# The fourth rotary embedding as four separate steps among the first half heads of the attention

## What is computed

```python
def rope_1d(x, pos):
    ...
    x1, x2 = x[..., :half], x[..., half:]
    return jnp.concatenate([x1 * cos - x2 * sin, x2 * cos + x1 * sin], axis=-1)

    qh = axial_rope(split_qk(q, S), row_pos, col_pos) * (DA_QK_DIM ** -0.5)
    kh = axial_rope(split_qk(k, S), row_pos, col_pos)
    k_all = jnp.concatenate([kh, split_qk(k_ctx, n_ctx)], axis=3)
    ...
        s = jnp.einsum('bhiqd,bhikd->bhiqk', qb, k_all).astype(jnp.float32)
        p = jax.nn.softmax(s, axis=-1)
        attn = p[:, :, 0] - lam * p[:, :, 1]
        return jnp.einsum('bhqk,bhkd->bhqd', attn.astype(v_all.dtype), v_all)
```

## Time and profile before

| | |
|---|---|
| median of three runs | 1947.11 us |
| lowest and highest | 1945.34 and 1947.85 us |
| the profiled execution, its own time | 1946.39 us |
| its span in the profile | 1944.6 us |
| instructions | 27546 |
| TensorE, VectorE, ScalarE busy | 98%, 72%, 50% of the span |

### The profile page before, as it was taken

One profiled execution on the slowest core, in us unless ns is written; L12 is line 12 of the kernel. 1 busy time (PEld: TensorE's weight loads), 2 busy tenths in 40 slices (PEclk: granted clock), 3 DMA queues, 4 the chain that ended last, 5 costly groups with the idle time before them and its releaser, 6 DMA issues.

```text
span 1944.6 us, 27546 instructions
## 1 busy us (share of the span) xinstructions
PE 1904.8 (98%) x10948; PEld 1640.9 (84%) x10948; DVE 1408.1 (72%) x1940; ACT 967.7 (50%) x1437; POOL 304.3 (16%) x490
## 2 busy tenths in 40 slices
PE   9999999999999999999999999999999999999998
PEld 8989898877888898977888888888888888888886
DVE  5686777764999989889878658666465677666665
ACT  6556566563544433444444455554443355545544
POOL 1025243342122222222221100100000000011000
PEclk9999999999999999999999999999999999999999
DMA  7455353544788888777887866765656544454563
GB/s 264 130 161 168 118 167 117 163 150 145 234 284 280 284 266 273 226 244 222 280 298 246 312 217 216 229 200 193 191 176 206 160 131 134 148 166 157 165 238 130
DMA packets 209233, 393.16 MB, mean 202 GB/s; under 512 B 12488, under 2 KB 61936, under 8 KB 207696
## 3 DMA queue, kind: packets, MB, share of 16 engines
q1 hardware_dynamic: 191248, 323.17, 50.8%
q0 software_dynamic: 17712, 68.17, 11.3%
q10 hardware_dynamic: 144, 0.07, 0.0%
HBM read 387.13 MB, written 4.23 MB: 201 GB/s over the span
## 4 chain that ended last, share of the span: by engine, by line
PE 83%; DVE 8%; issue 3%; ACT 3%; POOL 2%; DMA 1%; SPq 0%; DVEq 0%; ACTq 0%; POOLq 0%
PE GB L2121 44%; PE GB L2148 17%; PE GB L2133 9%; PE GB L2136 4%; DVE WL L2045 3%; DVE macc L1385 1%; PE SB L403 1%; ACT WH L2040 1%; PE SB L1693 1%; POOL XB L1069 1%; PE SB L1794 1%; PE SB L1685 1%; PE SB L1801 1%; POOL TB L1066 1%; PE SB L805 1%
## 5 line engine op out<-in xcount | busy, mean ns | idle before, releaser
L2045 DVE TENSOR_TENSOR WL<-raw,WH 128x1024 fp32r<-128x1024 f32 x605 | 729.8, 1231 | 194.8 <-ACT WH L2040 193.5
L2040 ACT ACTIVATE WH<-raw 128x1024 fp32r<-128x1024 f32 x605 | 621.7, 1057 | 295.4 <-PE GB L2121 160.5
L2121 PE MATMUL GB<-WH,uHL 128*128 128x512 f32 x1792 | 488.7, 395 | 3.6 <-DVE WL L2045 3.5
L2121 PEld LDWEIGHTS GB<-WH,uHL 128*128 128x128 f32 x1792 | 334.3, 189 | 74.9 <-DVE WL L2045 5.6
L2148 PE MATMUL GB<-uHL,WH 128*128 128x256 f32 x2048 | 294.5, 286 | 1.8 <-DVE uHL L439 1.6
L2121 PE MATMUL GB<-WH,hHL 128*128 128x512 f32 x1024 | 279.6, 395 | 0.4 <-issue 0.4
L2121 PE MATMUL GB<-WL,uHL 128*128 128x512 f32 x896 | 277.3, 391 | 0.0
L2148 PEld LDWEIGHTS GB<-uHL,WH 128*128 128x128 f32 x2048 | 264.6, 191 | 6.9 <-issue 3.4
L1385 DVE SCALAR_TENSOR_TENSOR macc<-wm,csil,macc 128x512 f32<-128x512 f32 x300 | 211.0, 751 | 37.5 <-DMA wm<-in_w_mod 36.2
L2121 PEld LDWEIGHTS GB<-WH,hHL 128*128 128x128 f32 x1024 | 190.5, 188 | 41.9 <-issue 3.4
L2121 PEld LDWEIGHTS GB<-WL,uHL 128*128 128x128 f32 x896 | 169.1, 189 | 35.9
(11 more groups left out here) (409 smaller groups left out, 1918.9 us busy)
## 6 DMA issues: line engine op xcount, KB each, us to landing
raw<-in_w_in SPq DMA_DIRECT2D x512, 512.0 KB, 4.6
wm<-in_w_mod POOLq DMA_DIRECT2D x96, 512.0 KB, 6.1
raw<-in_w_out SPq DMA_DIRECT2D x96, 512.0 KB, 5.1
xin<-in_x SPq DMA_DIRECT2D x4, 512.0 KB, 5.7
E<-decay_rows POOLq DMA_DIRECT2D x4, 512.0 KB, 4.7
hres<-in_x POOLq DMA_DIRECT2D x1, 2048.0 KB, 9.3
cin<-in_ctx POOLq DMA_DIRECT2D x1, 2048.0 KB, 11.9
h_spill<-hres POOLq DMA_DIRECT2D x2, 1024.0 KB, 5.1
```

Of the source, the lines that this page charges most:

```text
L2040: e.activation(place(s)[0][:, :, :], raw[s % NR][:, :, :], ACT.Copy).then_inc(*wh.inc("WH", s))
L2045: e.tensor_tensor(low[:, :, :], raw[s % NR][:, :, :], f32(high[:, :, :]), sub).then_inc(*wl.inc("WL", s))
L2121: m = e.matmul(banks[j][:, :], x[:, c, 128 * j:128 * j + 128], w[:, k, :], start=i == 0 and k == 0 and n == 0, stop=i == 7 and k == 1 and ...
```

## The change

The fourth rope gets four steps in place of one, in the slots +5, +7, +9 and +11, each on its own after TensorE's and VectorE's step of the attention in the slot before. The other three keep their slot: their four steps are called one right after the other. All four use the bias tile as scratch in place of `att`. TensorE's step 0 waits for rope 2 in place of rope 3, and its step 8, the first of head 4, waits for rope 3. GpSimd's first load of the bias waits for rope 3.

```diff
+ROPE, ROPE3 = (1, 1, 1, 1), (5, 7, 9, 11)
...
-        steps(("rope", k), end(kind, m) + 1, 1)
+        at(("rope", k), end(kind, m), ROPE if k < 3 else ROPE3)
...
-            turned = att[:, :, :].rearrange("p b (h t) -> p (b h) t", h=2)
+            turned = bias[:, :, :]
             e.stream_shuffle(turned, d, PARTNER).then_inc(*rp_dve.inc("x", k))
+            yield
             e.wait_ge(*rp_dve.at("x", k))
             e.tensor_tensor(turned, turned, sinT[:, :].unsqueeze(1).to_broadcast([128, 4, 256]),
                             mul).then_inc(*rp_dve.inc("s", k))
+            yield
             e.tensor_tensor(d, d, cosT[:, :].unsqueeze(1).to_broadcast([128, 4, 256]), mul).then_inc(*rp_dve.inc("c", k))
+            yield
             e.wait_ge(*rp_dve.at("c", k))
             e.tensor_tensor(d, d, turned, add).then_inc(*rp_dve.inc("r", k))
             yield
...
                 if n == 0:
+                    e.wait_ge(*rp_dve.at("r", 2))
+                    e.wait_ge(*kv_act.at("c", KV["vaX", 1]))
+                if n == 8:
                     e.wait_ge(*rp_dve.at("r", 3))
-                    e.wait_ge(*kv_act.at("c", KV["vaX", 1]))
...
                 if n >= 4:
                     e.wait_ge(*ab_dve.at(f"k{n - 4}"))
+                elif n == 0:
+                    e.wait_ge(*rp_dve.at("r", 3))
```

## The result

| | before | after |
|---|---|---|
| median of 11 runs each, side by side | 1946.4 us | 1942.0 us |
| lowest and highest | 1944.46 and 1948.57 us | 1940.04 and 1945.5 us |
| ratio | | 0.9981, 95% interval 0.9972 to 0.999 |
| span of the profiled execution | 1944.6 us | 1940.2 us |

The change is worth 0.19%, or 3.7 us with an interval of 1.9 to 5.5 us (0.0019, 0.001 and 0.0028 of 1946.4). The forecast was 3.4 us, so the gain fits it, and it lies just inside the bound of 0.2%. In absolute time the fit is less good: the forecast was 1943.7 us, and the measured median of 1942.0 us stands on the lower end of the range of 1942.0 to 1946.3 us. The two medians lie 4.4 us apart; the ratio with its interval is the fairer figure for the gain.

A forecast was written before the change was run, and what follows sets the result against it. PE was taken to bound the kernel, with its matmuls plus its pauses. Removing 2.45 + 1.43 = 3.88 us and adding 0.49 gives 3.39 us off the median 1947.11, so 1943.7 us; range 1942.0 to 1946.3 us.

The forecast's parts named there:

- The likeliest case: Step 0's pause and the clock's loss behind it go, half head 5 waits a little: 3.39 us gained, 45%.
- The pause of 2.45 us goes: At step 0, TensorE's scores no longer start late waiting for the fourth rope: 2.45 us gained.
- The clock gives back 1.43 us: Behind step 0's pause, the stretch that ran at a granted clock of 0.52 gets faster: 1.43 us gained.
- a rival of 22%: Behind step 0's pause, most executions don't pay the clock's 1.43 us: gain 1.96 us, 1945.2 us, chance 22%.
- Nothing takes the pause's place at step 0: At step 0, rope 2, splits and banks are ready early, so the whole 3.88 us go.
- T of half head 5 waits 0.49 us: VectorE's added rope instructions make step 5's maxima 1.45 us late, so PE waits 0.49 us at half head 5.
- the rival "all absorbed": VectorE's lateness stays under 0.96 us at half head 5: gain 3.88 us, 1943.2 us, chance 20%.
- A wait costs 0.12 us on VectorE: In the rope, an instruction waiting for its predecessor starts 1.26 us after it, one that doesn't 1.14 us.
- Splits, bias loads, the wait of step 8: nothing: Splits up to 1.5 us late, bias loads moved near 1591 us and step 8's wait for rope 3 cost nothing.
- The weight load's waits: From 1550 us on, its largest entry is eight waits for ACT, at most 0.4 us each, 2.7 us in all.
- The rival of the bound VectorE: VectorE becomes the bound, 4.67 us paid at T: 1952.2 us with clock falls, 1947.9 without; chance 8%.

The follow-up runs named there:

- the second repeat: The kernel before, unchanged, profiled again for the second of three more times: 1943.5 us.
- only the scratch: Against the changed kernel, fourth rope whole in slot +1 and step 0 waiting for it; new scratch and bias loads kept: 1942.6 us, one execution.

## Why the prediction was right

The likeliest case came true in its mechanism: the pause and the clock's loss behind it go, and a small wait at half head 5 comes. Part of the closeness is luck. The profile that the forecast started from had drawn a fall of the clock; and one term was 0.10 us too large and the other 0.34 us too large with the opposite sign. That the changed median stands on the end of the range is in part the start of the forecast: the kernel before measured 0.7 us less in eleven runs than in three. Step by step:

- *The pause of 2.45 us goes.* It did, with 2.35 us. The term was 0.10 too large: the step from the last pair to the scores takes 0.79 us, not the 0.69 between two pairs. Why it is longer isn't shown.
- *The clock gives back 1.43 us.* In the two profiles that were compared, yes. Over five profiles of that pause it is 0.90 us. The forecast set the whole term in its sum and kept the other outcome as a rival of 22% for "most executions"; what the five profiles show is a mixture. The sum for a typical execution would be 2.35 + 0.90 - 0.15 = 3.1 us, and the measured 3.7 (1.9 to 5.5) holds both that and the forecast's 3.4; the experiments can't tell them apart by time.
- *Nothing takes the pause's place at step 0.* Right; VectorE even idled 2.73 us ahead of the first maxima.
- *T of half head 5 waits 0.49 us.* Right in place, too large in size: 0.11 us, and 0.15 with the period behind it. The maxima of steps 2 to 5 were expected 0.07, 0.78, 0.74 and 1.45 us late. With the rows of after set 4.52 us later (T at 1576.77 against 1581.29 in the timeline of before), they are 0.11, 0.65, 0.53 and 1.06 late. The rows of before for this, the maxima of steps 1, 4 and 5, and ScalarE's instruction just ahead of step 3's copy at 1575.03:

```profile
1559.33 1.29 DVE L1733 TENSOR_REDUCE mxs<-SB 128x1 f32<-128x512 f32 x2
...
1583.91 1.29 DVE L1733 TENSOR_REDUCE mxs<-SB 128x1 f32<-128x512 f32 x2 [0.40 <-PE SB L1693]
...
1592.11 1.29 DVE L1733 TENSOR_REDUCE mxs<-SB 128x1 f32<-128x512 f32 x2 [0.40 <-PE SB L1693]
```

```profile
1574.80 0.19 ACT L1707 ACTIVATION_READ_ACCUMULATOR junk<-SB 128x1 f32 x1
```

  The parts that were taken too long are the hand-overs: 0.20 us from copy to maxima instead of 0.25, 0.67 from the keys' drain to the copy instead of 0.77 (in the row used, ScalarE's instruction ended at 1574.99, 0.04 us ahead of the copy, so the 0.10 were probably a wait for it), and 1.20 for the shuffle instead of 1.25. Against this stands an amount that the working left out: step 1's maxima, ahead of every rope instruction, are already 0.17 us late (1554.98 + 4.52 = 1559.50 against 1559.33). That comes with the clock staying up at step 0: they start 1.73 us behind T in the three profiles of the kernel before in which it fell, and 1.92 and 1.90 us behind it where it stayed (the second repeat, and only the scratch), as in the changed kernel (1.90). Without these 0.17 us the lateness at step 5 would be about 0.9 us, under the 0.96 us that cost nothing. So the rival "all absorbed" was missed by little.
- *A wait costs 0.12 us on VectorE.* The row of the chain has 1.25 us ahead of the instruction that waits (1564.25 to 1565.50 in the rope of one piece), the changed kernel 1.13 and 1.14 us on both sides of the same instruction between splits. The sentence of the Trainium skill, page "VectorE: DVE Perf Modes", section "The DRAIN you can't avoid", that the semaphore costs nothing extra, rests on eight copies in a row, and is not what these rows show for float32 products and a wait for the instruction just ahead. Spread, an instruction that had to wait in the chain costs 0.11 us less.
- *Splits, bias loads, the wait of step 8: nothing.* TensorE's list of waits is empty from 1540 us on, and so all three were covered. The loads were expected near 1591 and stand at 1587.03, right behind the rope as expected.
- *The weight load's waits.* The prediction calls the eight waits for ScalarE, 2.7 us in all, the largest entry between 1550 us and the end. They are the largest with a releaser; an entry for which the profile names none is larger, 3.0 us, 8 times, at most 0.7. Nothing in the sum hangs on it, and the third stretches above show that the gain reaches the end.

The rival of the bound VectorE did not come true in any placement. It said that the idle times can't be used and that all 4.67 us are paid at T; even in one lump, where the chain takes 4.9 us, T waits 2.89. What it had right is that the clock can fall behind such a pause: it did behind 2.89 us and not behind the two of under 1 us.

## What to carry to other kernels

Work of a helper engine that is not wanted at once should go piece by piece into the periods in which that engine has spare time, and the spare time is read from its own timeline: idle ahead of the instruction that starts the next hand-over, plus the slack between the hand-over and its use. Here 4.9 us of work cost 0.15 us in four pieces, 1.8 us in two pairs, and 2.9 us in one lump, which the clock's fall made 4.5. A gain that includes the clock's recovery should be priced over several profiles, since one shows only one draw.

## What was not expected of the hardware

- TensorE's clock behind a pause of 2.27 or 2.28 us went down to the lower level in three of five profiles and stayed at 1.00 in two, with the same instructions ahead of it. At the pause of 2.36 to 2.38 us near 124 us the same matmuls took 2.08 us in three of ten profiles, the changed kernel's among them, and 1.12 or 1.13 us in the other seven. Near 450 us it fell in all ten. Each fall at step 0 cost 1.43 to 1.55 us. Behind the pauses of 0.7 to 1.1 us in the experiments it never fell. The Trainium skill, page "TensorE: Matmul & The Clock Gate", section "Part 1: The HAM clock gate (the "warmup" mystery)", says that the watching of activity is not tied to the kernel's start; the mixture agrees with that, though no run here shows the cause, nor why the place near 450 us is not mixed.
- Times of one kernel scatter by some us: such falls at several pauses are a likely part, not shown as such, of why 25 runs of the kernel before lie between 1942.11 and 1951.06 us. In the ten profiles the spread of 5 us was there at the first write of the spilled residual, and the 298 us behind it agreed to 0.02 us.
